# Narrow norms of the differential tiles, the widest block of the latent maps scaled on ScalarE, and another order of head work

## The reference

```python
def second_block(x, mem, positions, ...):
    h = rms_norm(x, norm_g[l])
    proj = h @ w_in[l]
    cq, ckv, kr, dq, dk, dv, mq, z = jnp.split(proj, IN_OFFSETS_2, axis=-1)
    y_mla = mla_branch(cq, ckv, kr, positions, ...)      # 8 heads, scores of 96 features
    y_diff = diff_branch(dq, dk, dv, positions, ...)     # 4 heads, two maps each
    y_mem = mem_branch(mq, mem, ...)                     # 4 heads, 256 memory tokens
    y = jnp.concatenate([y_mla, y_diff, y_mem], axis=-1) * jax.nn.silu(z)
    return x + y @ w_out[l]

def diff_branch(...):
    ...
        p = jax.nn.softmax(sc, axis=-1)
        a = (p[:, :, 0] - lam * p[:, :, 1]).astype(v.dtype)
        return jnp.einsum('bhqk,bkhd->bqhd', a, v)
    o = causal_block_sweep(block_fn, q)
    o = rms_norm(o, subln_g) * (1.0 - lam_init)          # over the 64 features of a head
    return o.reshape(b, s, DIFF_W)
```

## Time and profile before

| what | us |
|---|---|
| median of 3 runs | 1208.46 |
| the runs | 1206.82, 1208.46, 1214.39 |
| the profiled execution | 1208.47 |
| its span, from the first to the last instruction | 1206.7 |
| PE busy | 1107.4 (92% of the span) |
| DVE busy | 661.0 (55%) |
| ACT busy | 579.1 (48%) |
| POOL busy | 391.5 (32%) |

### The profile page before, as it was taken

One profiled execution on the slowest core, in us unless ns is written; L12 is line 12 of the kernel. 1 busy time (PEld: TensorE's weight loads), 2 busy tenths in 40 slices (PEclk: granted clock), 3 DMA queues, 4 the chain that ended last, 5 costly groups with the idle time before them and its releaser, 6 DMA issues.

```text
span 1206.7 us, 15719 instructions
## 1 busy us (share of the span) xinstructions
PE 1107.4 (92%) x5254; PEld 923.9 (77%) x5254; DVE 661.0 (55%) x1521; ACT 579.1 (48%) x1168; POOL 391.5 (32%) x172
## 2 busy tenths in 40 slices
PE   6899899899999999999999999998996888967888
PEld 4778688799878787888888888887875766756777
DVE  4537456888644565554454432242565756686941
ACT  5344457888624344444444434243443436565631
POOL 1245453000134443444444444344432431000013
PEclk9999899899999999999999999998998896587999
DMA  5353342011024332322232243233421221000113
GB/s 193 87 173 115 109 152 88 19 36 36 27 88 136 109 101 74 105 87 104 87 104 89 102 139 105 87 105 105 145 82 53 88 70 53 1 1 18 36 64 110
DMA packets 35315, 105.04 MB, mean 87 GB/s; under 512 B 5771, under 2 KB 7947, under 8 KB 34571
## 3 DMA queue, kind: packets, MB, share of 16 engines
q1 hardware_dynamic: 24732, 85.50, 21.3%
q10 hardware_dynamic: 10528, 18.83, 5.0%
HBM read 99.99 MB, written 7.70 MB: 89 GB/s over the span
## 4 chain that ended last, share of the span: by engine, by line
issue 65%; POOL 16%; PE 11%; DVE 5%; DMA 1%; POOLq 1%; ACT 1%; ACTq 0%
POOL WLO L568 16%; PE PS L1653 3%; PE PS L1654 3%; PE PS L1655 3%; PE PS L1817 1%; DVE PB L1194 1%; DVE HLO L1109 1%; DMA X<-xT 1%; DVE PB L1229 1%; DVE PB L1314 1%; DVE BLO L1109 1%; POOLq L564 0%; DVE PS L1308 0%; POOLq L567 0%; ACT PB L760 0%
## 5 line engine op out<-in xcount | busy, mean ns | idle before, releaser
L568 POOL TENSOR_TENSOR WLO<-RAW,WHI 128x1024 fp32r<-128x1024 f32 x160 | 389.1, 2433 | 803.9 <-ACT WHI L582 803.7
L582 ACT ACTIVATE WHI<-RAW 128x1024 fp32r<-128x1024 f32 x162 | 171.6, 1059 | 311.9 <-PE PS L1655 295.8
L1653 PE MATMUL PS<-HHI,WHI 128*128 128x512 f32 x648 | 260.8, 402 | 30.9 <-POOL WLO L568 21.5
L1654 PE MATMUL PS<-HLO,WHI 128*128 128x512 f32 x648 | 257.0, 397 | 0.0
L1655 PE MATMUL PS<-HHI,WLO 128*128 128x512 f32 x648 | 256.8, 396 | 0.0
L1653 PEld LDWEIGHTS PS<-HHI,WHI 128*128 128x128 f32 x648 | 124.7, 192 | 62.9 <-issue 26.2
L1653 PE MATMUL PS<-BHI,WHI 128*128 128x512 f32 x368 | 146.2, 397 | 2.4 <-DVE BLO L1109 1.3
L1655 PEld LDWEIGHTS PS<-HHI,WLO 128*128 128x128 f32 x648 | 124.4, 192 | 26.8
L1654 PEld LDWEIGHTS PS<-HLO,WHI 128*128 128x128 f32 x648 | 125.0, 193 | 25.8 <-issue 0.5
L1654 PE MATMUL PS<-BLO,WHI 128*128 128x512 f32 x368 | 144.0, 391 | 0.0
L1655 PE MATMUL PS<-BHI,WLO 128*128 128x512 f32 x368 | 144.0, 391 | 0.0
(11 more groups left out here) (285 smaller groups left out, 1772.9 us busy)
## 6 DMA issues: line engine op xcount, KB each, us to landing
RAW<-wstream SPq DMA_DIRECT2D x162, 512.0 KB, 3.2
X<-xT ACTq DMA_DIRECT2D x4, 512.0 KB, 9.7
bias_b<-bias_rows ACTq DMA_DIRECT2D x2, 1024.0 KB
...
```

The lines of the kernel that those rows point to most:

```text
L568: pool.tensor_tensor(WLO[:, s, :], RAW[:, s, :], WHI[:, s, :].bitcast(F), ALU.subtract).then_inc(split_lo, 1)
L582: act.activation(WHI[:, c % 2, :], RAW[:, c % 2, :], ACT.Copy).then_inc(split_hi, 1)
L1653: pe.matmul(dst, a[0], b[0], start=first, stop=False, **kw)
L1654: pe.matmul(dst, a[0], b[1], start=False, stop=False, **kw)
```

## The change

It has three parts.

1. **Norm of the differential tiles.** PE makes the sums with the tile as the weights and two columns of BONE as the moving part: 4 matmuls of 128x2, with tokens on rows and a column per head. DVE scales and inverts 128x8 into SS instead of 128x512 in place. ACT's root reads SS, each column 64 times, and writes 128x512. Then 4 new matmuls by the identity (the spread) turn it back into a PSUM bank (5 or 6), and the product reads it there. The product now waits for the spread (`dm_spread`), and the values that use that bank next wait for the product (`dm_read`).
2. **Latent maps.** The widest block (the last 128 queries, 128x512) is scaled by ACT with Copy instead of DVE, behind the exponential of the next map; PE's transposes of this block wait for `wide_last`. 8 instructions go from DVE to ACT.
3. **Order of the head work.** On DVE `head_norm(5)` and `head_turned(5)` stand ahead of `z_scale(7)` and `head_lo(4)`, `mla_turned(6)` comes after `head_lo(5)` and `z_scale(2)`, and the last gate blocks are taken in another order. On ACT some roots, high parts, weight copies and the two stores of X (`x_keep`) change places. On PE uk6 stands ahead of z0, z4 ahead of z3 and z5 ahead of z6, with z5 in another bank.

The diff, cut to its core:

```diff
...
 NPOS, NU = NU, NU - 2
-TAIL_UNITS = "c0 c1 c2 c3 d0 d1 d2 u4 d3 m0 m1 m2 u5 m3 z7 z0 uk6 z2 z1 uk7 z3 z4 z6 z5 ukv".split()
+TAIL_UNITS = "c0 c1 c2 c3 d0 d1 d2 u4 d3 m0 m1 m2 u5 m3 z7 uk6 z0 z2 z1 uk7 z4 z3 z5 z6 ukv".split()
 STORED = "c0 c1 c2 c3 d0 d1 d2 d3 m0 m1 m2 m3 z0 z1 z2 z3 z4 z5 z6 z7 u4 u5 ukv".split()
...
                 m["g1"], m["t1"] = ng, nt
-                m["n0"] = m["t0"] - max(0, i - 8) if maps is ab else m["t0"]
+                m["n0"] = m["t0"] - max(0, i - 8) if maps is ab else m["t0"] - i if maps is mla else m["t0"]
                 m["i"], m["prev"] = i, maps[i - 1]
...
 
-        DIFF_BANK = [m["bank"] for m in dm if m.get("diff") and m["last"] and m["h"] % 2]
+        DIFF_BANK = [6, 5]
 
...
                     if tile is not None:
-                        act.wait_ge(dm_rin, 2 * tile + 2)
-                        act.activation(YSQ, YSQ, ACT.Sqrt).then_inc(dm_rstd, 1)
+                        act.wait_ge(dm_rin, tile + 1)
+                        act.activation(YSQ.rearrange("p (g e) -> p g e", g=8), SS[:, 0:8, None].broadcast_to([P, 8, 64]),
+                                       ACT.Sqrt).then_inc(dm_rstd, 1)
                     if 0 <= i - 1 < len(maps) and maps[i - 1].get("mode") != "hold":
...
                             bias_load(m["bias"] + 1)
+                    if name == "mla" and 0 <= i < len(maps):
+                        m = maps[i]
+                        act.wait_ge(A["normed"], m["n0"] + 1)
+                        wide_ap = prob_of(m, 3)
+                        act.activation(wide_ap, wide_ap, ACT.Copy, scale=stat(m, WT)[:, 3:4]).then_inc(wide_last, 1)
                     if name == "ab" and 8 <= i < len(maps):
...
             head_hi(0)
+            act.wait_ge(x_fin, 4)
+            act.dma_start(x_keep[:, 0:4, :], X[:, 0:4, :]).then_inc(x_out, 16)
             stream(UNIT["mem"] + 9)
...
             head_square(1)
-            act.wait_ge(x_fin, 4)
-            act.dma_start(x_keep[:, 0:4, :], X[:, 0:4, :]).then_inc(x_out, 16)
             head_root(1)
...
             stream(UNIT["mem"] + 11)
+            head_hi(1)
             act.wait_ge(x_fin, 8)
             act.dma_start(x_keep[:, 4:8, :], X[:, 4:8, :]).then_inc(x_out, 16)
-            head_hi(1)
             stream(UNIT["mem"] + 12)
...
             stream(UNIT["mem"] + 20)
+            head_root(5)
             head_hi(4)
-            head_root(5)
             stream(UNIT["mem"] + 21)
...
             mla_squares(6)
+            head_root(6)
             stream(UNIT["mem"] + 22)
-            head_root(6)
             stream(UNIT["mem"] + 23)
...
             head_root(7)
+            stream(UNIT["mem"] + 27)
             head_hi(7)
-            stream(UNIT["mem"] + 27)
             stream(UNIT["mem"] + 28)
...
                 act.activation(FX[:, z, :], FX[:, z, :], ACT.Silu).then_inc(z_done, 1)
+            stream(UNIT["mem"] + 29)
             used(tail("ukv"))
...
                 act.activation(hi(LV[tk]), PS[:, (4, 5, 6, 7)[tk], :], ACT.Copy).then_inc(vm_hi, 1)
-            stream(UNIT["mem"] + 29)
             attention("dm")
...
                     link(dve.tensor_tensor(stat(m, WT), stat(m, WT), LAM[:, 0:1].broadcast_to([P, NT]), ALU.mult))
-                for qs in m["groups"][:2] if "ks" in m else m["groups"]:
+                for qs in m["groups"][:2] if "ks" in m or m["scale"] == 96 ** -0.5 else m["groups"]:
                     for q in qs:
...
                     if tile is not None:
-                        dve.wait_ge(dm_rstd, tile + 1)
-                        link(dve.scalar_tensor_tensor(out=YT, in0=YT, scalar=col("subln"), in1=YSQ,
-                                                      op0=ALU.mult, op1=ALU.mult))
+                        dve.wait_ge(dm_spread, tile + 1)
+                        dve.scalar_tensor_tensor(out=YT, in0=YT, scalar=col("subln"), in1=PS[:, DIFF_BANK[tile], :],
+                                                 op0=ALU.mult, op1=ALU.mult).then_inc(dm_read, 1)
+                        dve.wait_ge(dm_read, tile + 1)
                         dve.scalar_tensor_tensor(out=YT, in0=YT, scalar=1.0 - LAM_INIT, in1=FX[:, 4 + tile, :],
...
                         dve.wait_ge(dm_tot, tile + 1)
-                        dve.tensor_scalar(YSQ, PS[:, DIFF_BANK[tile], :], 1.0 / 64, EPS, ALU.mult, ALU.add).then_inc(dm_rin, 1)
-                        dve.wait_ge(dm_rin, 2 * tile + 1)
-                        dve.reciprocal(YSQ, YSQ).then_inc(dm_rin, 1)
+                        link(dve.tensor_scalar(SS[:, 0:8], PS[:, DIFF_BANK[tile], 0:8], 1.0 / 64, EPS, ALU.mult, ALU.add))
+                        dve.reciprocal(SS[:, 0:8], SS[:, 0:8]).then_inc(dm_rin, 1)
 
...
             mla_turned(4)
+            head_norm(5)
+            head_turned(5)
             z_scale(7, 0)
             head_lo(4)
-            head_norm(5)
-            head_turned(5)
             mla_norm(6)
             z_scale(0, 1)
-            mla_turned(6)
             head_lo(5)
             z_scale(2, 7)
+            mla_turned(6)
             z_scale(1, 6)
...
             mla_turned(7)
+            z_scale(4, 1)
             z_scale(3, 0)
-            z_scale(4, 1)
+            z_scale(5, 0)
+            head_lo(7)
             z_scale(6, 3)
-            head_lo(7)
-            z_scale(5, 2)
             for tk in range(NT):
...
                         pe.wait_ge(wide, m["i"] - 7)
+                    elif m["scale"] == 96 ** -0.5 and g == 2:
+                        pe.wait_ge(wide_last, m["i"] + 1)
                     else:
...
                             pe.wait_ge(A["y_lo"], before["yf"])
-                        elif before["h"] % 2:
-                            pe.wait_ge(dm_rin, 2 * (before["h"] // 2) + 1)
+                        elif before["h"] % 2 and m["bank"] == DIFF_BANK[before["h"] // 2]:
+                            pe.wait_ge(dm_read, before["h"] // 2 + 1)
                         else:
...
                         pe.wait_ge(dm_sq, tile + 1)
-                        pe.matmul(PS[:, DIFF_BANK[tile], :], BONE[:, :], YSQ, start=True, stop=True,
-                                  skip_group_check=True).then_inc(dm_tot, 1)
+                        for tk in range(NT):
+                            ins = pe.matmul(PS[:, DIFF_BANK[tile], 2 * tk:2 * tk + 2], YSQ[:, tk * P:(tk + 1) * P], BONE[:, 0:P:64],
+                                            start=True, stop=True, skip_group_check=True)
+                        ins.then_inc(dm_tot, 1)
+                    if diff_tile(maps, i - 4) is not None:
+                        tile = diff_tile(maps, i - 4)
+                        pe.wait_ge(dm_rstd, tile + 1)
+                        for tk in range(NT):
+                            ins = pe.matmul(PS[:, DIFF_BANK[tile], tk * P:(tk + 1) * P], YSQ[:, tk * P:(tk + 1) * P],
+                                            IDN[:, :], start=True, stop=True, skip_group_check=True)
+                        ins.then_inc(dm_spread, 1)
                     if 0 <= i - 1 < len(maps) and maps[i - 1].get("mode") != "hold":
...
             head_turn(4)
-            pe.wait_ge(*tok_at(5, 2))
-            unit_T(tail("z0"), 1, H).then_inc(unit_used, 1)
             pe.wait_ge(*tok_at(5, 4))
...
             key_part(6, "uk6")
+            pe.wait_ge(*tok_at(5, 2))
+            unit_T(tail("z0"), 1, H).then_inc(unit_used, 1)
             pe.wait_ge(h_lo, 5)
...
             head_turn(6)
+            pe.wait_ge(scaled, SCALED["z"] + 2)
+            unit_T(tail("z4"), 1, H).then_inc(unit_used, 1)
             pe.wait_ge(scaled, SCALED["z"] + 1)
             unit_T(tail("z3"), 0, H).then_inc(unit_used, 1)
-            pe.wait_ge(scaled, SCALED["z"] + 2)
-            unit_T(tail("z4"), 1, H).then_inc(unit_used, 1)
             head_turn(7)
+            pe.wait_ge(scaled, SCALED["z"] + 6)
+            unit_T(tail("z5"), 0, H).then_inc(unit_used, 1)
             pe.wait_ge(*tok_at(7, 4))
             unit_T(tail("z6"), 3, H).then_inc(unit_used, 1)
-            pe.wait_ge(*tok_at(7, 2))
-            unit_T(tail("z5"), 2, H).then_inc(unit_used, 1)
             pe.wait_ge(h_lo, 8)
...
             pe.wait_ge(scaled, SCALED["z"] + 8)
+            pe.wait_ge(*tok_at(7, 2))
             pe.wait_ge(vm_lo, 4)
```

6 lines of the change are left out of this document (3 added, 3 removed).

## The result

| kernel | median, us | lowest to highest | runs |
|---|---|---|---|
| before | 1208.84 | 1206.82 to 1214.39 | 8 |
| changed | 1201.56 | 1197.52 to 1205.17 | 8 |

The ratio is 0.9934, with a 95% interval of 0.9909 to 0.9960: the change is faster by 0.7%, where 1200.6 us and "within 1%" were forecast. That they add up so well is luck.

A forecast was written before the change was run, and what follows sets the result against it. With PE busy 92% of the span, the prediction looked for its idle times. Its terms −2.5 (heads), −1.2 (tile 0), −1.3 (tile 1) and −2.9 (latent maps) make −7.9 against 1208.47: 1200.6 us, range 1190 to 1208.5.

The forecast's parts named there:

- heads: Head stage: the new order removes 4.05 us of PE waits and adds 0.7 and 0.8, so −2.5, bounds 0 and −4.05.
- tile 0: Differential norm, first tile: DVE saves 3.65 us, but the product waits for PE's spread; −1.2, bounds 0 and −2.3.
- tile 1: Differential norm, second tile: ACT's root comes 2.03 us sooner, the spread takes 0.7; −1.3, bounds −0.7 and −2.0.
- latent maps: Six of eight maps each lose a 0.482 us scaling from DVE, ACT having time to spare; −2.9, bounds 0 and −3.9.
- the circle: Head stage: head_norm(5) on DVE stands behind head_lo(4), which waits for ACT; opening it removes PE's 3.52 us wait ahead of z2.
- the stream copy stands after head_hi(4) at about 945 to 946: Head stage, ACT: the weight copy moves there from 949.53, so POOL's 2.64 us split ends near 949.
- The swap: PE runs uk6 before z0, 1.6 us against 5.6; claimed to cost a new wait taken as 0.7 us.
- the wait behind uk7: Head stage: PE's 1.59 us wait for weights grows by 0.8, since ACT's copy stays behind work that DVE feeds.
- the spread: Differential tiles: PE's four new transposes, priced at 0.19 us each, 0.7 in all, behind 12 score matmuls at tile 0.
- rival C: Slower: the clock doesn't rise at 1055.2, so 12.5 us of PE work takes twice as long, 1213.1; chance 0.08.
- Rival E: Latent maps: the scaling on ACT becomes a wait and the −2.9 goes, 1203.5; chance 0.05.
- Rival D: The clock stays high from 1007.4 to 1055.2, saving at most 16.7 us, some 15: 1186; chance 0.13.

The follow-up runs named there:

- e4: Changed kernel with PE's four spread matmuls moved ahead of the scores of the map two on, at tile 0: 1194.99 us, ratio 0.9899.
- e7: Changed kernel with the spread issued as PE's transpose instead of a float32 matmul by the identity, at the same place: 1201.09 us, ratio 0.9936.
- e10: Changed kernel with the 128x384 block of each latent map scaled on ACT too: 1197.70 us, ratio 0.9903.
- e8: Changed kernel with ACT's copy of z3's weights ahead of head_hi(6) and the squares of group 7: 1203.81 us, ratio 0.9962.
- e1: Kernel before with the new order of head work alone: 1201.71 us, ratio 0.9964.
- e2: Kernel before with the narrow norm of the differential tiles alone: 1208.97 us, ratio 1.0007.
- e3: Kernel before with the widest block of the latent maps scaled on ACT alone: 1204.89 us, ratio 0.9985.
- e5: Kernel before with only head_norm(5), head_turned(5) ahead of z_scale(7), head_lo(4) on DVE and head_root(5) ahead of head_hi(4) on ACT: 1203.53 us, ratio 0.9963.

## Why the forecast held, term by term

| term | forecast | traces |
|---|---|---|
| heads | −2.5 | −4.6 in the profiled execution and in e4; −0.5 and −0.7 in e7 and e10 with the same order, −0.9 in e8; −8.0 in e1, 2.6 of it not from the edit |
| tile 0 | −1.2 | +0.7 (e2) |
| tile 1 | −1.3 | −0.7 (e2); −0.3 in the changed kernel |
| latent maps | −2.9 | −2.9 (e3), about 2.3 of it from the scaling; −3.0 in the changed kernel |
| clock in maps 5 and 6 | 0 | −4.6 where the head stage is 169.3 us or shorter, 0 where it is longer |

**Heads.** Mis-sized, and for a mis-told reason. What the sum called the circle is 1.2 (e5); the step "the stream copy stands after head_hi(4) at about 945 to 946" holds only with uk6 ahead of z0, since otherwise the copy waits for z0 until 948.4. The swap was booked as a cost of 0.7 and is the other half. The second term that was missing is the clock: the unit behind the 3.52 us wait ran at 1.2 GHz before and doesn't now, which is the other 2.6 of z2's 5.2 (3.52 − 0.35 − 0.67 = 2.5 is the wait). The third is DVE's chain to head_turn(7): before, PE waited 1.99 there, which the prediction doesn't name, and in the changed kernel's trace 0.39. The gain of 5.2 still shrinks to 4.6 by the end of the stage: the clock is low for 3.4 us in z3's unit, and again from 1003.1, 3.2 us ahead of the first bias. And the wait behind uk7 isn't there for DVE's sake: e8 shows that ACT's place of the copy makes it, and that DVE's chain to head_turn(7) stands right behind. PE's row of before, to set beside the changed kernel's at 985.48:

```profile
987.19 1.95 PE L1986 MATMUL PS<-IDN,PB 128*96 128x128 f32 x16 [1.99 <-DVE PB L1560]
```

**Tile 0.** The step that failed is the spread: 0.7 taken from PE's transposes, where it is 2.07. The form, a float32 matmul by the identity, makes about half of this (e7: 1.11 as a transpose), and the low clock about half too (at tile 1, at the high one, it is 1.16). As the change holds no transposes of PE's own kind, what rival C says of them doesn't bear on it. The scores behind which the spread stands are 2.86, at the top of the range given. From the start of the sum to the product it is 1064.93 − 1056.01 = 8.9 us, against 8.2 before.

**Tile 1.** The root came where it was expected, behind its table load, but the spread took 1.16 at the high clock. This is ACT's row and PE's of the changed kernel, answering to the earlier trace rows:

```profile
1091.73 0.63 ACT L719 ACTIVATE PB<-SS 128x512 f32<-128x512 f32 x1
...
1092.41 1.16 PE L1892 MATMUL PS<-IDN,PB 128*128 128x128 f32 x8 [1.72 <-ACT PB L719]
```

The Trainium skill's page "FP8 and Floating Point Precision", section "TensorE Precision Notes", says that true float32 takes four passes. The trace doesn't show four: it has two records for each matmul by the identity and one for each transpose, and 2.07 us against 1.11 for the four of them.

**Latent maps.** Right in the mechanism: DVE's floor sinks in each map that waits for nothing else, and the first two give nothing (1.65 and 8.47 us before and now). The size is 0.40 a map and not the 0.482 that the instruction takes by itself: DVE's instructions overlap here, so what one takes out of the pace is less than its duration (before, the scaling of 128x384 lasts 0.41 us and the one behind it starts 0.33 after it). Six times 0.40 is 2.4; that 2.9 to 3.0 came is luck, by the 0.65 of the third map. Rival E didn't come; e10 shows where it begins, one block further on.

**The clock.** Rival D came true in part. The low stretch of 47.8 us shrank to 34, and two maps that no edit touches took 9.6 us in place of 14.2. In all six traces whose head stage is 169.3 us or shorter they take 9.6, in all eight with 171.8 or more 14.2, with none between. So in these traces about 4.6 us more go with a short head stage than its own waits. This is a correlation over 14 executions of different kernels, and not a cause shown by an edit; the shorter runs of the kernel before, at a higher mean clock, have no trace, and they may have the 9.6 as well. What decides the level stays open. Rival C came in part too: behind tile 0 the changed kernel has the low clock for 27.3 us, where the kernel before had 10.2 and then, later, 3.4.

**The total.** −4.6 (heads) − 2.5 (maps: the clock's 4.6 less 2.0 given back in the map behind tile 0) − 3.0 (latent) + 2.7 (ahead of the stage, scatter) = −7.4. The forecast of −7.9 was near by luck: the head order and the clock gave more and the norm nothing, in this execution. The changed kernel's eight runs lie at 1197.5 to 1198.2 (three) and 1201.1 to 1205.2 (five). That these are the two courses of the head stage is not shown: the profiled execution kept the head gain and is one of the five, 2.7 us late ahead of the stage.
